# Second RMS norm of a one-core hybrid layer: token sums on partitions, formed by small products behind each output block, in place of a 128-wide sum, root and reciprocal after the last one

## The chip, the cores and the metric

One NeuronCore of one Trainium2 chip runs the whole step as one program. The metric is the device time of that program in microseconds, lower is better; it is the median of several executions. Engines are named as in the profile: PE (TensorE, with PEld its weight loads), DVE (VectorE), ACT (ScalarE), POOL (GpSimd), SP (SyncE, which issues most transfers).

## The reference

The kernel computes one layer on 1024 latent and 128 context tokens of width 1024. The part that matters here is the second norm between the mixer's output projection and the feed-forward:

```python
def rms_norm(x, g):
    xf = x.astype(jnp.float32)
    y = xf * lax.rsqrt(jnp.mean(xf * xf, axis=-1, keepdims=True) + EPS)
    return (y * g.astype(jnp.float32)).astype(x.dtype)
...
    x = x + gt1 * mix                       # mix ends with @ p['w_o']
    xn = rms_norm(x, p['norm2_g']) * (1.0 + sc2) + sh2
    x = x + gt2 * (jnp.square(jax.nn.relu(xn @ p['w_ff1'])) @ p['w_ff2'])
```

Everything is float32.

## The kernel before

Activations lie transposed: channels on the 128 partitions (`KT = 8` blocks of 128 channels), the `T = 1152` tokens along the free dimension, which PE takes in `G = 3` groups of `GN = 384`. `NC = 9` is the number of 128-token chunks. A float32 product is made of three single-pass products on planes of type fp32r: a plane `hi` (the rounded value) and `lo` (the rest), as hi·hi, hi·lo and lo·hi. Weights are split the same way, one 128x1024 block at a time: ACT writes `hi` (L1464, `high`), POOL subtracts to get `lo` (L693, `low`), PE waits for `wl_ok`.

`wave3` (L1149) is one output block: 3 groups of 24 matmuls with 384 columns each, into six PSUM banks used in turn (`WAVE = 6`); banks 6 and 7, which the profile calls `ser`, are free in this stage. The stage concerned has three parts:

1. **Output projection.** Eight output blocks m. After each group DVE adds the gated result to the residual (L1940, writes `x2`). After a block ACT squares it into `sq2[:, m % 2]` (L1490), and DVE adds that to `acc` [128 x 1152] (L1944).
2. **Root.** After the last block PE multiplies `acc` by a matrix of ones, one matmul a group (L1194), which leaves each token's sum on all 128 partitions. ACT takes the root (L1493), DVE the reciprocal of the full 128x1152 tile `rs2` (L1946).
3. **Normalised planes.** For each channel block m: DVE multiplies `x2` by `rs2` (L1953, `xs_ok`), ACT applies scale and shift (L1497, `raw2_ok`) and rounds to `xn2_hi` (L1501, `n2hi_ok`), DVE subtracts to get `xn2_lo` (L1950, `norm_low`, `n2_ok`). `first_hidden` (L1195) on PE takes block k as soon as `n2_ok` reaches k+1: 9 matmuls a block, against the first feed-forward weight block. Then `wave3` goes on with the second weight block, which needs `wl_ok` again.

The order on every engine is the order of the code; there is no scheduler. POOL, in this stage, makes the `lo` plane of one weight block for each output block, then waits for `sum_full`, issues the load of the last norm's weights `gf` (L714) and goes on with `low` for the second feed-forward block.

SBUF tiles that alias are named in the trace by their carrier: `sq2`, `acc`, `rs2`, `gf`, `hsq` appear as `gts`, `xn2_hi`, `xn2_lo`, `xn2_raw` as `xn_hi`, `xn_lo`, `xn_raw`, and the banks as `gbank`, `bank`, `inv`, `ser`, in this order, two of each.

Of the kernel before, what the change touches and what calls it, by code (L numbers as in the profile page):

```python
# [66 lines left out]
N_BRANCH = KT  # L67
# [127 lines left out]
def flow_step(nc, xs, xp, wblocks, pack, packl, vecs, csil_in, consts, gfin, y_out, yp_out, st_out):  # L195
    ctx = ExitStack()
    with ctx:
# [13 lines left out]
        banks = [gbank[:, 0, :], gbank[:, 1, :]]  # L211
# [6 lines left out]
        def sb(st, name, shape, dt=F32):  # L218
            return st.enter_context(nc.sbuf_tensor(name, shape, dt))
# [3 lines left out]
        ident = sb(ctx, "ident", [P, P])  # L223
        bones = sb(ctx, "bones", [P, P])
        ones = sb(ctx, "ones", [P, P])
# [3 lines left out]
        eps_t = sb(ctx, "eps_t", [P, 2])  # L229
# [40 lines left out]
        def sub_tmp(p, d, n, m):  # L270
# [48 lines left out]
        xn2_hi = sb(later, "xn2_hi", [P, KT, T], F32R)  # L319
        x2 = sb(later, "x2", [P, KT, T])  # L320
        xn2_raw = sb(later, "xn2_raw", [P, KT, T])
# [8 lines left out]
        mix_hi = sb(planes, "mix_hi", [P, KT, T], F32R)  # L330
        xa_hi = sb(planes, "xa_hi", [P, KT, T], F32R)
        xn2_lo = sb(planes, "xn2_lo", [P, KT, T], F32R)
        planes.close()
        fin = ExitStack()
# [3 lines left out]
        mix_lo = sb(fin, "mix_lo", [P, KT, T], F32R)  # L338
        gts = sb(fin, "gts", [P, 2, 2, T])
# [4 lines left out]
        sq2 = gts[:, :, 0, :]  # L344
        rs2 = gts[:, 0, 1, :]
        hsq = gts[:, 0, 0, 0:2 * GN].rearrange("p (q t) -> p q t", q=2)
        acc = gts[:, 1, 1, :]
        gf = gts[:, 1, 1, 0:D]
        gate_slots = gts[:, :, :, :].rearrange("p a b t -> p (a b) t")
        yo = xb[:, :, :].rearrange("p k t -> p (k t)")  # L350
        squares = mix_raw[:, :, :].rearrange("p k t -> p (k t)")
        fss = sb(fin, "fss", [P, NC, 2])
        frs = sb(fin, "frs", [P, NC])
        fin.close()
# [6 lines left out]
            tr_full tc_ok p1_full p1_ok dt_full xt_ok tt_ok xtb_ok  # L361
            ur_full ur_ok u_full u_ok s_full y_full s_ok ya_ok yd_ok sf_ok sf_out pl_in0 pl_in1
            mu_full yc_ok ysq_ok var_full std_ok rec_ok spread_full gate_full xa_ok xa_out0 xa_out1 ada_full mrow_ok mt_full ada_ok
            dve_chain pool_chain a_in b_in gt_in0 gt_in1 gt_in2 gt_in3 xh_ok xl_ok xt_in0 xt_in1 wh_ok wl_ok o_full o_free raw_ok hi_ok mix_ok sq_ok acc_ok
            sum_full rs_a2 xs_ok raw2_ok n2hi_ok n2_ok hsq_ok hhi_ok h_ok fin_full fin_sq fin_sum fin_std fin_free fin_out gf_in""".split()
        S = {n: ctx.enter_context(nc.semaphore(n)) for n in names}
        w_full = [ctx.enter_context(nc.semaphore(f"w_full{s}")) for s in range(RING)]
        bon_in = [ctx.enter_context(nc.semaphore(f"bon_in{s}")) for s in range(5)]
# [2 lines left out]
        MIX_FILLS, WO_FILLS, FF_FILLS = 6 * KT, 3 * KT, 3 * (HB + KT)  # L371
# [6 lines left out]
        def cols(cg):  # L378
            return slice(cg * GN, (cg + 1) * GN)
# [234 lines left out]
        def _(pool):  # L614
            ch = Chain(pool, S["pool_chain"])
# [92 lines left out]
            for m in range(KT):  # L708
# [1 line left out]
                    pool.wait_ge(S["o_free"], WAVE + MIX_FILLS + G * m)  # L710
                    pool.dma_start(xts[:, (m + 1) % 2, :], xt_d[m + 1]).then_inc(S[f"xt_in{(m + 1) % 2}"], 16)
                low(2 * N_BRANCH + m + 1)
            pool.wait_ge(S["sum_full"], G)
            pool.dma_start(gf[:], gfin).then_inc(S["gf_in"], 16)  # L714
            with pool.Fori(0, FFE - 1) as i:
                for b in range(2 * HB):
# [11 lines left out]
        def _(pe):  # L728
            def mm(out, lhsT, rhs, start, stop):
                return nc.tensor.matmul(out, lhsT, rhs, start=start, stop=stop)  # L730
# [30 lines left out]
            for c in range(KT):  # L761
                for cg in range(G):
# [3 lines left out]
                    for i in range(G):  # L766
                        ins = nc.tensor.transpose(banks[n % WAVE][:, i * P:(i + 1) * P], x0[:, cg * G + i, c * P:(c + 1) * P], ident[:])
# [5 lines left out]
            for b in range(N_ADA_FIRST):  # L773
                ins = mm(banks[6][:, 2 * b:2 * b + 2], mrow1[:, b // 4, (b % 4) * P:(b % 4 + 1) * P], sel[:], True, True)
# [3 lines left out]
            for c in range(KT):  # L778
                for cg in range(G):
# [4 lines left out]
                    for i in range(G):  # L784
                        ins = nc.tensor.transpose(banks[n % WAVE][:, i * P:(i + 1) * P], xnrm[:, cg * G + i, c * P:(c + 1) * P], ident[:])
# [48 lines left out]
            for k in range(KT):  # L834
                pe.wait_ge(S["xlo_pool" if k % 2 else "xlo_dve"], k // 2 + 1)
                for cg in range(G):
                    ins = product3(banks[FL.bank("l", 0, cg)][:, :GN], *wsp[0], k, cg)
# [7 lines left out]
            for p in range(PAIRS):  # L845
# [7 lines left out]
                for name in AFTER:  # L853
# [10 lines left out]
                    else:  # L864
                        pe.wait_ge(ev["A"], FL.emptied(p, "v")[1])
                        for cg in range(G):
                            o = free_bank(p, name, cg)
                            for i in range(G):
                                t = G * cg + i
                                ins = nc.tensor.transpose(o[:, i * P:(i + 1) * P], vf[:, t * C:(t + 1) * C], ident[:])  # L870
# [278 lines left out]
            def wave3(n0, it, per_it, b, per_b, ks, x, tail=0, ready=None):  # L1149

                if tail == 0:
                    pe.wait_ge(S["wl_ok"], it * per_b + (b + 1))
                hi, lo = wsp[b % 2]
                for cg in range(G):
                    n = n0 + cg
                    pe.wait_ge(S["o_free"], it * per_it + n + 1)
                    if ready:
                        pe.wait_ge(S[ready[0]], it * ready[1] + (ready[2] + cg + 1))
                    for k, kw in enumerate(ks):
                        o = banks[n % WAVE][:, :GN]  # L1160
                        mm(o, hi[:, kw, :], x[0][:, k, cols(cg)], k == 0, False)
                        mm(o, hi[:, kw, :], x[1][:, k, cols(cg)], False, False)
                        ins = mm(o, lo[:, kw, :], x[0][:, k, cols(cg)], False, k == len(ks) - 1)
                    ins.then_inc(S["o_full"], 1)
# [19 lines left out]
                    b = N_BRANCH * x + m  # L1184
                    wave3(G * b, 0, 0, b, 0, range(KT), planes_x)
            pe.wait_ge(S["mix_ok"], G * KT)
            with pe.Fori(0, KT // 4) as i:
                for s in range(4):
                    wave3(MIX_FILLS + 3 * s, i, 12, 2 * N_BRANCH + s, 4, range(KT), (mix_hi, mix_lo))
            n_ff = MIX_FILLS + WO_FILLS  # L1190
            pe.wait_ge(S["o_free"], WAVE + n_ff)
            pe.wait_ge(S["acc_ok"], KT + 1)
            for cg in range(G):
                mm(banks[cg][:, :GN], ones[:], acc[:, cols(cg)], True, True).then_inc(S["sum_full"], 1)  # L1194
            def first_hidden():  # L1195

                pe.wait_ge(S["wl_ok"], 2 * N_BRANCH + KT + 1)
# [24 lines left out]
            for t in range(NC):  # L1222
                if t >= 3:
                    pe.wait_ge(S["fin_free"], 2 * (t - 3) + 2)
                for c in range(KT):
                    ins = nc.tensor.transpose(banks[2 * (t % 3) + c // 4][:, (c % 4) * P:(c % 4 + 1) * P], x2[:, c, t * P:(t + 1) * P], ident[:])
# [5 lines left out]
        def _(act):  # L1232
            A = nc.scalar.activation
# [251 lines left out]
            for m in range(KT):  # L1485
                high(2 * N_BRANCH + m + 1, before=MIX_FILLS + G * m)
                act.wait_ge(S["o_free"], WAVE + MIX_FILLS + G * (m + 1))
                if m >= 2:
                    act.wait_ge(S["acc_ok"], m)
                A(sq2[:, m % 2, :], x2[:, m, :], ACT.Square).then_inc(S["sq_ok"], 1)  # L1490
            for cg in range(G):
                act.wait_ge(S["sum_full"], cg + 1)
                A(rs2[:, cols(cg)], banks[cg][:, :GN], ACT.Sqrt, scale=1.0 / D, bias=eps_t[:, 0:1]).then_inc(S["rs_a2"], 1)  # L1493
            for m in range(KT):
                act.wait_ge(S["xs_ok"], m + 1)
                for a, b, kind in ((0, LAT, 0), (LAT, T, 1)):
                    ins = A(xn2_raw[:, m, a:b], xn2_raw[:, m, a:b], ACT.Identity,  # L1497
                            scale=mul2[:, m, kind:kind + 1], bias=mods[:, 24 + m, kind:kind + 1])
                ins.then_inc(S["raw2_ok"], 1)
                act.wait_ge(S["raw2_ok"], m + 1)  # L1500
                A(xn2_hi[:, m, :], xn2_raw[:, m, :], ACT.Copy).then_inc(S["n2hi_ok"], 1)  # L1501

            n_ff = MIX_FILLS + WO_FILLS

# [27 lines left out]
        def _(dve):  # L1532
            V = nc.vector
            ch = Chain(dve, S["dve_chain"])
# [393 lines left out]
                            if m or cg:  # L1928
                                mix_low(*divmod(G * m + cg - 1, G))
            mix_low(KT - 1, G - 1)  # L1930
            V.memset(acc, 0.0).then_inc(S["acc_ok"], 1)
            with dve.Fori(0, KT // 4) as i:
                for s in range(4):
                    m = 4 * i + s
                    dve.wait_ge(S[f"xt_in{s % 2}"], 32 * i + 16 * (s // 2) + 16)
                    for cg in range(G):
                        n = MIX_FILLS + 3 * s + cg
                        dve.wait_ge(S["o_full"], 12 * i + (n + 1))
                        for a, b, kind in kinds(cg):
                            ins = stt(x2[:, m, a:b], banks[n % WAVE][:, a - cg * GN:b - cg * GN], hgt1[:, m, kind:kind + 1], xts[:, s % 2, a:b], mul, add)  # L1940
                        ins.then_inc(S["o_free"], 1)
                    dve.wait_ge(S["sq_ok"], 4 * i + s + 1)
                    dve.wait_ge(S["acc_ok"], 4 * i + s + 1)
                    V.tensor_tensor(acc, acc, sq2[:, s % 2, :], add).then_inc(S["acc_ok"], 1)  # L1944
            dve.wait_ge(S["rs_a2"], G)
            ch.step(V.reciprocal(rs2, rs2))  # L1946
            ch.settle()
            def norm_low(m):
                dve.wait_ge(S["n2hi_ok"], m + 1)
                V.tensor_tensor(xn2_lo[:, m, :], xn2_raw[:, m, :], xn2_hi[:, m, :].bitcast(F32), sub).then_inc(S["n2_ok"], 1)  # L1950

            for m in range(KT):
                V.tensor_tensor(xn2_raw[:, m, :], x2[:, m, :], rs2, mul).then_inc(S["xs_ok"], 1)  # L1953
                if m >= 2:
                    norm_low(m - 2)
            norm_low(KT - 2)
            norm_low(KT - 1)
            n_ff = MIX_FILLS + WO_FILLS

            def hidden_low(it, n):  # L1960
# [136 lines left out]
```

## Time and profile before

| | us |
|---|---|
| median of 3 runs (lowest to highest) | 2875.52 (2867.75 to 2883.12) |
| the profiled execution, its own time | 2867.05 |
| its span in the trace | 2865.1 |
| PE busy in the span | 2712.8 (95%) |
| DVE, ACT, POOL busy | 1442.3, 823.7, 739.7 |

The span leaves out about 2 us around the first and last instruction. Mean granted TensorE clock is 0.979 of full. The output projection runs from 1904.3 to 2006.4 us of the span, the root and the planes from there to about 2050, the feed-forward from there almost to the end.

### The profile page before, as it was taken

How to read it: one execution, taken by the hardware profiler on the slowest of the kernel's cores; microseconds unless marked ns; L12 is line 12 of the kernel's file. 1: busy time of each engine (PE TensorE's matmuls, PEld its weight loads, DVE VectorE, ACT ScalarE, POOL GpSimd, SP SyncE). 2: the span in 40 equal slices, each digit the busy share in tenths (PEclk: the TensorE clock that was granted, in tenths of full speed). 3: DMA queues.
4: the chain of work that ended last, by engine and by line, in shares of the span. 5: the costliest groups of instructions: out<-in, count | busy, mean ns of one | idle time of the engine just before them, and what ended most of it. 6: DMA issues, size and time to landing. Idle time of an engine off the chain costs nothing.

```text
span 2865.1 us, 65324 instructions
## 1 busy us (share of the span) xinstructions
PE 2712.8 (95%) x27766; PEld 2543.0 (89%) x27766; DVE 1442.3 (50%) x2754; ACT 823.7 (29%) x1542; POOL 739.7 (26%) x883
## 2 busy tenths in 40 slices
PE   3899999999999979999999989999699999999997
PEld 2799999999999967778888879999699999999996
DVE  1355665655845725776666651542633333333334
ACT  3344243343342413333333330211411111111112
POOL 0311111111211215555555532212122212211221
PEclk8899999999999989999999999999899999999999
DMA  7324425425335254444444552212011111111101
GB/s 297 100 69 138 138 72 177 135 68 176 108 103 153 79 169 122 132 122 140 135 136 142 155 209 97 89 50 81 30 45 45 37 44 44 44 37 44 44 29 66
DMA packets 276308, 293.76 MB, mean 103 GB/s; under 512 B 76128, under 2 KB 215776, under 8 KB 275936
## 3 DMA queue, kind: packets, MB, share of 16 engines
q1 hardware_dynamic: 267104, 254.54, 28.9%
q0 software_dynamic: 7200, 28.84, 2.7%
q10 hardware_dynamic: 1760, 6.82, 0.6%
q8 instruction: 191, 3.13, 0.4%
q14 instruction: 53, 0.43, 0.0%
HBM read 198.76 MB, written 91.36 MB: 101 GB/s over the span
## 4 chain that ended last, share of the span: by engine, by line
PE 92%; issue 3%; DVE 3%; DMA 2%; ACT 1%; SPq 1%; POOL 0%; DVEq 0%; POOLq 0%; ACTq 0%
PE gbank L730 26%; PE inv L730 23%; PE bank L730 23%; PE ser L730 17%; PE inv L916 1%; DMA ring<-in_wblocks 1%; PE bank L903 1%; DVE gmat L1756 1%; DMA xt_d<-xt_s 0%; DVE xr L1588 0%; DVE xb L1993 0%; POOL wsp L693 0%; SPq L543 0%; SPq L544 0%; DVE yf L1816 0%
## 5 line engine op out<-in xcount | busy, mean ns | idle before, releaser
L693 POOL TENSOR_TENSOR wsp<-ring,wsp 128x1024 fp32r<-128x1024 f32 x88 | 215.8, 2453 | 842.2 <-ACT wsp L1464 819.1
L624 POOL TENSOR_TENSOR wsp<-ring,wsp 128x1024 fp32r<-128x1024 f32 x67 | 174.8, 2609 | 746.7 <-ACT wsp L1260 746.7
L730 PE MATMUL gbank<-xn_hi,wsp 128*128 128x384 f32 x1312 | 348.3, 339 | 18.9 <-DVE xn_lo L1950 18.2
L730 PE MATMUL bank<-xn_hi,wsp 128*128 128x384 f32 x1312 | 345.3, 337 | 0.4 <-POOL wsp L693 0.4
L730 PE MATMUL inv<-xn_hi,wsp 128*128 128x384 f32 x1312 | 343.5, 337 | 0.0
L730 PEld LDWEIGHTS gbank<-xn_hi,wsp 128*128 128x128 f32 x1312 | 239.5, 189 | 23.7 <-issue 15.7
L730 PEld LDWEIGHTS bank<-xn_hi,wsp 128*128 128x128 f32 x1312 | 238.3, 188 | 2.5 <-POOL wsp L693 0.7
L730 PEld LDWEIGHTS inv<-xn_hi,wsp 128*128 128x128 f32 x1312 | 237.9, 188 | 1.8 <-POOL wsp L624 1.1
L1464 ACT ACTIVATE wsp<-ring 128x1024 fp32r<-128x1024 f32 x88 | 92.6, 1052 | 465.0 <-PE inv L730 385.5
L730 PE MATMUL ser<-xn_hi,wsp 128*128 128x384 f32 x816 | 218.8, 342 | 5.4 <-DVE xr L1588 5.4
L730 PE MATMUL bank<-xn_lo,wsp 128*128 128x384 f32 x656 | 220.5, 336 | 1.4 <-issue 1.4
L730 PE MATMUL gbank<-xn_lo,wsp 128*128 128x384 f32 x656 | 221.1, 337 | 0.0
L730 PE MATMUL inv<-xn_lo,wsp 128*128 128x384 f32 x656 | 220.3, 336 | 0.0
L730 PE MATMUL gbank<-ub 64*64 64x128 f32 (+1 forms) x3456 | 183.1, 316 | 21.4 <-DVE gmat L1756 12.4
L1756 DVE TENSOR_TENSOR gmat<-gbank,gmask 128x1024 f32<-128x1024 f32 x144 | 175.4, 1218 | 44.8 <-PE gbank L730 44.8
L730 PE MATMUL gbank<-mix_lo,wsp 128*128 128x384 f32 x832 | 159.9, 335 | 0.0
L730 PE MATMUL inv<-mix_lo,wsp 128*128 128x384 f32 x832 | 159.9, 335 | 0.0
L730 PE MATMUL bank<-mix_lo,wsp 128*128 128x384 f32 x832 | 159.9, 335 | 0.0
L730 PEld LDWEIGHTS ser<-xn_hi,wsp 128*128 128x128 f32 x816 | 150.5, 190 | 7.4 <-DVE xr L1588 5.6
L730 PEld LDWEIGHTS bank<-mix_lo,wsp 128*128 128x128 f32 x832 | 145.6, 188 | 0.0
L730 PEld LDWEIGHTS inv<-mix_lo,wsp 128*128 128x128 f32 x832 | 145.6, 188 | 0.0
L730 PEld LDWEIGHTS gbank<-mix_lo,wsp 128*128 128x128 f32 x832 | 145.6, 188 | 0.0
(380 smaller groups left out, 5295.0 us busy)
## 6 DMA issues: line engine op xcount, KB each, us to landing
ring<-in_wblocks SPq DMA_DIRECT2D x195, 512.0 KB, 3.6
ub<-op_d SPq DMA_DIRECT2D x144, 256.0 KB, 2.8
op_d<-ar SPq DMA_DIRECT2D x32, 576.0 KB, 5.4
op_d<-bk SPq DMA_DIRECT2D x32, 576.0 KB, 6.2
vb<-v_d SPq DMA_DIRECT2D x144, 64.0 KB, 3.0
xt_d<-xt_s POOLq DMA_DIRECT2D x8, 576.0 KB, 3.2
x_d<-zero SPq DMA_DIRECT2D x8, 576.0 KB, 6.8
v_d<-vn SPq DMA_DIRECT2D x8, 576.0 KB, 6.8
```

Source lines behind the costliest of these rows:

```text
L624: GT(wsp[s % 2][1][:], ring[(N_ADA_RING + s) % RING][:], wsp[s % 2][0][:].bitcast(F32), ALU.subtract).then_inc(S["wsplit_lo"], 1)
L693: nc.gpsimd.tensor_tensor(wsp[b % 2][1][:], ring[(N_MIX0 + b) % RING][:], wsp[b % 2][0][:].bitcast(F32), ALU.subtract).then_inc(S["wl_ok"], 1)
L730: return nc.tensor.matmul(out, lhsT, rhs, start=start, stop=stop)
L903: ins = nc.tensor.transpose(banks[3][:, y * P:(y + 1) * P], ub[v % LOADS][:, y // 2, 2 + y % 2, :], ident[:])
L916: ins = nc.tensor.transpose(inv[:, 0, x * P:(x + 1) * P], xt[:, place_of(v), :, :].rearrange("p h t -> p (h t)"), ident[:])
L1464: A(wsp[b % 2][0][:], ring[slot][:], ACT.Copy).then_inc(S["wh_ok"], 1)
L1756: V.tensor_tensor(gmat[v % SETS][:, d, :, :, :].rearrange("p h x t -> p h (x t)"), gbank[:, :, :], gmask[:, d:d + 1, :].to_broadcast([P, 2 ...
```

## The change

- The squares of block m are no longer added up by DVE. PE multiplies each 128-token chunk of `sq2` (as the stationary operand) by two columns of ones: nine matmuls a block, accumulated over the eight blocks in bank 6, which leave the sum of token p of chunk t on partition p in column 2t (`token_sums`). They stand one block behind: the sums of block m-1 come after the matmuls of block m. PE's loop of two turns is written out.
- ACT takes the root of those nine columns (128x9) and DVE the reciprocal of 128x9 (`rtok`).
- PE spreads `rtok` back over partitions: nine matmuls with a column of `rtok` repeated 128 times as stationary operand and the identity as moving one, into banks 3 to 5; ACT copies these to `rs2`.
- The rounding to `xn2_hi` is done by ACT for even m and by DVE (`norm_high`) for odd m; the subtraction to `xn2_lo` is done by POOL for all m. The load of `gf` on POOL stands behind these eight subtractions.

```diff
-        acc = gts[:, 1, 1, :]
+        rtok = sb(fin, "rtok", [P, NC])
...
-            pool.wait_ge(S["sum_full"], G)
+            for m in range(KT):
+                pool.wait_ge(S["n2hd_ok" if m % 2 else "n2hi_ok"], m // 2 + 1)
+                nc.gpsimd.tensor_tensor(xn2_lo[:, m, :], xn2_raw[:, m, :], xn2_hi[:, m, :].bitcast(F32), ALU.subtract).then_inc(S["n2_ok"], 1)
             pool.dma_start(gf[:], gfin).then_inc(S["gf_in"], 16)
...
-            with pe.Fori(0, KT // 4) as i:
-                for s in range(4):
-                    wave3(MIX_FILLS + 3 * s, i, 12, 2 * N_BRANCH + s, 4, range(KT), (mix_hi, mix_lo))
+            def token_sums(m):
+
+                pe.wait_ge(S["sq_ok"], m + 1)
+                for t in range(NC):
+                    ins = mm(banks[6][:, 2 * t:2 * t + 2], sq2[:, m % 2, t * P:(t + 1) * P], ones[:, 0:2], m == 0 and t == 0, m == KT - 1 and t == NC - 1)
+                ins.then_inc(S["ss_full"], 1)
+
+            for m in range(KT):
+                wave3(MIX_FILLS + 3 * m, 0, 0, 2 * N_BRANCH + m, 0, range(KT), (mix_hi, mix_lo))
+                if m:
+                    token_sums(m - 1)
+            token_sums(KT - 1)
             n_ff = MIX_FILLS + WO_FILLS
             pe.wait_ge(S["o_free"], WAVE + n_ff)
-            pe.wait_ge(S["acc_ok"], KT + 1)
+            pe.wait_ge(S["rtok_ok"], 1)
             for cg in range(G):
-                mm(banks[cg][:, :GN], ones[:], acc[:, cols(cg)], True, True).then_inc(S["sum_full"], 1)
+                for i in range(G):
+                    t = G * cg + i
+                    ins = mm(banks[3 + cg][:, i * P:(i + 1) * P], rtok[:, t:t + 1].to_broadcast([P, P]), ident[:], True, True)
+                ins.then_inc(S["sum_full"], 1)
...
                 if m >= 2:
-                    act.wait_ge(S["acc_ok"], m)
+                    act.wait_ge(S["ss_full"], m - 1)
                 A(sq2[:, m % 2, :], x2[:, m, :], ACT.Square).then_inc(S["sq_ok"], 1)
+            act.wait_ge(S["ss_full"], KT)
+            A(rtok[:], banks[6][:, 0:2 * NC:2], ACT.Sqrt, scale=1.0 / D, bias=eps_t[:, 0:1]).then_inc(S["rs_a2"], 1)
             for cg in range(G):
                 act.wait_ge(S["sum_full"], cg + 1)
-                A(rs2[:, cols(cg)], banks[cg][:, :GN], ACT.Sqrt, scale=1.0 / D, bias=eps_t[:, 0:1]).then_inc(S["rs_a2"], 1)
+                A(rs2[:, cols(cg)], banks[3 + cg][:, :GN], ACT.Copy).then_inc(S["rs_ok"], 1)
...
-                act.wait_ge(S["raw2_ok"], m + 1)
-                A(xn2_hi[:, m, :], xn2_raw[:, m, :], ACT.Copy).then_inc(S["n2hi_ok"], 1)
+                if m % 2 == 0:
+                    act.wait_ge(S["raw2_ok"], m + 1)
+                    A(xn2_hi[:, m, :], xn2_raw[:, m, :], ACT.Copy).then_inc(S["n2hi_ok"], 1)
...
-                    V.tensor_tensor(acc, acc, sq2[:, s % 2, :], add).then_inc(S["acc_ok"], 1)
-            dve.wait_ge(S["rs_a2"], G)
-            ch.step(V.reciprocal(rs2, rs2))
-            ch.settle()
-            def norm_low(m):
-                dve.wait_ge(S["n2hi_ok"], m + 1)
-                V.tensor_tensor(xn2_lo[:, m, :], xn2_raw[:, m, :], xn2_hi[:, m, :].bitcast(F32), sub).then_inc(S["n2_ok"], 1)
-
+            dve.wait_ge(S["rs_a2"], 1)
+            V.reciprocal(rtok[:], rtok[:]).then_inc(S["rtok_ok"], 1)
+            def norm_high(m):
+                dve.wait_ge(S["raw2_ok"], m + 1)
+                V.tensor_copy(xn2_hi[:, m, :], xn2_raw[:, m, :]).then_inc(S["n2hd_ok"], 1)
+
+            dve.wait_ge(S["rs_ok"], G)
             for m in range(KT):
                 V.tensor_tensor(xn2_raw[:, m, :], x2[:, m, :], rs2, mul).then_inc(S["xs_ok"], 1)
-                if m >= 2:
-                    norm_low(m - 2)
-            norm_low(KT - 2)
-            norm_low(KT - 1)
+                if m >= 3 and m % 2:
+                    norm_high(m - 2)
+            norm_high(KT - 1)
```

How this moves instructions is seen best on three engines. On PE, where one output block ends and the next begins, the changed program has (the first row is the last product of a block, `ones,gts` are the token sums):

```order
L732 MATMUL inv<-mix_lo,wsp 128x384
L732 MATMUL inv<-mix_hi,wsp 128x384
L732 MATMUL ser<-ones,gts 128x2 x9
L732 MATMUL gbank<-mix_hi,wsp 128x384
L732 MATMUL gbank<-mix_lo,wsp 128x384
```

Before, the row of nine is not there and the next block follows at once. Such a row of nine stands between two blocks six times (the sums of blocks 0 to 5, each behind the block after it). The sums of blocks 6 and 7 stand together behind the last block:

```order
L732 MATMUL inv<-mix_hi,wsp 128x384
L732 MATMUL ser<-ones,gts 128x2 x18
L732 MATMUL bank<-ident,rtok 128x128 x3
L732 MATMUL inv<-ident,rtok 128x128 x6
L732 MATMUL gbank<-xn_hi,wsp 128x384
```

where before there stand the three matmuls of the ones matrix:

```order
L730 MATMUL gbank<-gts,ones 128x384 x2
L730 MATMUL bank<-gts,ones 128x384
L730 MATMUL gbank<-xn_hi,wsp 128x384
```

On DVE after the last residual add, first before and then changed (`xn_raw<-x,gts` are the multiplications by the root's reciprocal, `CAST` is `norm_high`):

```order
L1946 RECIPROCAL gts<-gts 128x1152
L1953 TENSOR_TENSOR xn_raw<-x,gts 128x1152 x3
L1950 TENSOR_TENSOR xn_lo<-xn_raw,xn_hi 128x1152
L1953 TENSOR_TENSOR xn_raw<-x,gts 128x1152
```

```order
L1960 RECIPROCAL rtok<-rtok 128x9
L1967 TENSOR_TENSOR xn_raw<-x,gts 128x1152 x4
L1963 CAST xn_hi<-xn_raw 128x1152
L1967 TENSOR_TENSOR xn_raw<-x,gts 128x1152 x2
L1963 CAST xn_hi<-xn_raw 128x1152
L1967 TENSOR_TENSOR xn_raw<-x,gts 128x1152 x2
L1963 CAST xn_hi<-xn_raw 128x1152 x2
```

The subtractions have left DVE and four casts stand there. On POOL, ahead of the second feed-forward weight block, the changed program has:

```order
L715 TENSOR_TENSOR xn_lo<-xn_raw,xn_hi 128x1152 x8
L716 DMA gts<-in_gfin 128x1024
L717 UNCONDITIONAL_BRANCH
L717 ISA
L693 TENSOR_TENSOR wsp<-ring,wsp 128x1024
```

Before, the DMA and the L693 row stand there without the eight subtractions.

## Rows read from the trace of the kernel before

**Rows 1.** The page: the span.
```profile
span 2865.1 us, 65324 instructions
```
**Rows 2.** Stretches: us; busy PE, PEld, DVE, ACT, POOL (instructions); clock, DMA share, GB/s.
```profile
1904.30:2006.40 102.10, 102.02 (x576) 101.70 (x576) 25.53 (x38) 14.89 (x15) 24.13 (x14) 1.00 0.23 76
...
2008.00:2050.00 42.00, 21.37 (x83) 16.93 (x84) 32.01 (x21) 25.21 (x30) 3.16 (x2) 0.72 0.04 13
```
**Rows 3.** Timeline of PE, 2006 to 2050: start, length, instruction, idle before.
```profile
2006.05 0.34 PE L730 MATMUL inv<-mix_hi,wsp 128*128 128x384 f32 x1
...
2010.02 2.90 PE L730 MATMUL gbank<-gts,ones 128*128 128x384 f32 x4 [3.63 <-DVE gts L1944]
2012.72 1.49 PE L730 MATMUL bank<-gts,ones 128*128 128x384 f32 x2
...
2049.14 0.44 PE L730 MATMUL bank<-xn_hi,wsp 128*128 128x384 f32 x1 [0.40 <-POOL wsp L693]
```
**Rows 4.** Timelines of ACT and DVE, 2006 to 2050.
```profile
2007.32 1.16 ACT L1490 ACTIVATE gts<-x 128x1152 f32<-128x1152 f32 x1 [10.61 <-DVE x L1940]
2011.68 0.58 ACT L1493 ACTIVATE gts<-gbank,eps_t 128x384 f32<-128x384 f32 x1 [3.20 <-PE gbank L730]
...
2026.36 1.61 ACT L1497 ACTIVATE xn_raw<-xn_raw,mods,mul 128x1024 f32<-128x1024 f32 x2
2028.00 1.17 ACT L1501 ACTIVATE xn_hi<-xn_raw 128x1152 fp32r<-128x1152 f32 x1
...
2014.86 7.35 DVE L1946 RECIPROCAL gts<-gts 128x1152 f32<-128x1152 f32 x1 [4.98 <-ACT gts L1493]
2022.24 3.89 DVE L1953 TENSOR_TENSOR xn_raw<-x,gts 128x1152 f32<-128x1152 f32 x3
...
2045.49 1.36 DVE L1950 TENSOR_TENSOR xn_lo<-xn_raw,xn_hi 128x1152 fp32r<-128x1152 f32 x1 [1.36 <-ACT xn_hi L1501]
```
**Rows 5.** Timeline of POOL, 2006 to 2075.
```profile
2014.50 0.57 POOL L714 DMA_DIRECT2D gts<-in_gfin  x1 [15.08 <-PE bank L730]
...
2053.87 2.40 POOL L693 TENSOR_TENSOR wsp<-ring,wsp 128x1024 fp32r<-128x1024 f32 x1 [4.78 <-ACT wsp L1464]
```
**Rows 6.** Float32 matmuls of two columns: eight weight loads; PE and clock in the prologue's.
```profile
1190.85 0.97 PEld L730 LDWEIGHTS bank<-sel,mrow 128*128 128x128 f32 x8 [0.17 <-issue]
...
70.00:73.00 3.00, 3.00 (x28) 1.00 0.19 75
73.00:73.50 0.50, 0.50 (x6) 0.71 0.00 0
...
76.50:77.00 0.50, 0.50 (x6) 0.88 0.00 0
```
**Rows 7.** Small operations like the added ones: ACT and DVE on 128x9.
```profile
L1303 ACT ACTIVATE emid<-mid 128x9 f32<-128x9 f32 x16 | 3.1, 193 | 0.0
...
L1558 DVE RECIPROCAL rs<-rs x1: 205/205/205, 43.5 to 43.5; 128x9 f32<-128x9 f32 x1
```
**Rows 8.** PE's clock after its last output matmul (windows of 0.5 us).
```profile
2008.50:2009.00 0.50, 0.00 (x0) 0.57 0.00 0
```
**Rows 9.** Timelines of POOL, then of DVE, in the prologue.
```profile
81.35 2.63 POOL L629 TENSOR_TENSOR xn_lo<-xr,xn_hi 128x1152 fp32r<-128x1152 f32 x1 [12.78 <-DVE xr L1588]
83.94 3.47 POOL L624 TENSOR_TENSOR wsp<-ring,wsp 128x1024 fp32r<-128x1024 f32 x1
...
83.17 2.02 DVE L1579 TENSOR_TENSOR xn_lo<-xr,xn_hi 128x1152 fp32r<-128x1152 f32 x1
```
**Rows 10.** A DVE cast, and a DVE op with one SBUF input (min/median/max ns).
```profile
L1566 DVE CAST gmask<-cst x1: 686/686/686, 50.1 to 50.1; 128x1024 bf16<-128x1024 f32 x1
...
L1701 DVE TENSOR_SCALAR kk<-kk x8: 760/761/762, 186.4 to 976.2; 128x1152 f32<-128x1152 f32 x8
```
**Rows 11.** DVE's timeline where POOL's split of 803.03 to 805.42 runs.
```profile
803.03 2.39 POOL L624 TENSOR_TENSOR wsp<-ring,wsp 128x1024 fp32r<-128x1024 f32 x1 [13.95 <-ACT wsp L1260]
...
803.92 1.52 DVE L1612 TENSOR_SCALAR half<-pk 128x4 f32<-128x4 f32 x1
```

More of the change, by code:

```diff
@@ L363, in flow_step @@
             mu_full yc_ok ysq_ok var_full std_ok rec_ok spread_full gate_full xa_ok xa_out0 xa_out1 ada_full mrow_ok mt_full ada_ok
-            dve_chain pool_chain a_in b_in gt_in0 gt_in1 gt_in2 gt_in3 xh_ok xl_ok xt_in0 xt_in1 wh_ok wl_ok o_full o_free raw_ok hi_ok mix_ok sq_ok acc_ok
-            sum_full rs_a2 xs_ok raw2_ok n2hi_ok n2_ok hsq_ok hhi_ok h_ok fin_full fin_sq fin_sum fin_std fin_free fin_out gf_in""".split()
+            dve_chain pool_chain a_in b_in gt_in0 gt_in1 gt_in2 gt_in3 xh_ok xl_ok xt_in0 xt_in1 wh_ok wl_ok o_full o_free raw_ok hi_ok mix_ok sq_ok ss_full
+            sum_full rs_a2 rtok_ok rs_ok xs_ok raw2_ok n2hi_ok n2hd_ok n2_ok hsq_ok hhi_ok h_ok fin_full fin_sq fin_sum fin_std fin_free fin_out gf_in""".split()
         S = {n: ctx.enter_context(nc.semaphore(n)) for n in names}
@@ L1930, in _ @@
             mix_low(KT - 1, G - 1)
-            V.memset(acc, 0.0).then_inc(S["acc_ok"], 1)
             with dve.Fori(0, KT // 4) as i:
@@ L1941, in _ @@
                         ins.then_inc(S["o_free"], 1)
-                    dve.wait_ge(S["sq_ok"], 4 * i + s + 1)
-                    dve.wait_ge(S["acc_ok"], 4 * i + s + 1)
-                    V.tensor_tensor(acc, acc, sq2[:, s % 2, :], add).then_inc(S["acc_ok"], 1)
-            dve.wait_ge(S["rs_a2"], G)
-            ch.step(V.reciprocal(rs2, rs2))
-            ch.settle()
-            def norm_low(m):
-                dve.wait_ge(S["n2hi_ok"], m + 1)
-                V.tensor_tensor(xn2_lo[:, m, :], xn2_raw[:, m, :], xn2_hi[:, m, :].bitcast(F32), sub).then_inc(S["n2_ok"], 1)
+            dve.wait_ge(S["rs_a2"], 1)
[4 more added lines that the diff above has]
+            dve.wait_ge(S["rs_ok"], G)
             for m in range(KT):
                 V.tensor_tensor(xn2_raw[:, m, :], x2[:, m, :], rs2, mul).then_inc(S["xs_ok"], 1)
-                if m >= 2:
-                    norm_low(m - 2)
-            norm_low(KT - 2)
-            norm_low(KT - 1)
+                if m >= 3 and m % 2:
+                    norm_high(m - 2)
+            norm_high(KT - 1)
             n_ff = MIX_FILLS + WO_FILLS
```

## The prediction

> **What bounds the kernel now.** I read the table of stretches first. Over the eight output blocks PE is busy 102.02 of 102.10 us, at full clock, and its weight loads 101.70; DVE, ACT and POOL are under a quarter [rows 2]. So in this stretch each microsecond of PE work lengthens the kernel by one, and work taken from DVE is worth nothing. In the next one PE is busy for half of the time and its clock is at 0.72: here a chain through the other engines sets the end. I then read that chain in the timelines, with t = 0 at the end of PE's last output matmul, 2006.05 + 0.34 = 2006.39 [rows 3]:
> - The last block is squared by 2008.48, t = 2.1 [rows 4]; DVE adds it, PE starts on the ones matrix at 2010.02 [rows 3].
> - ACT takes three roots, and DVE the reciprocal from 2014.86, 7.35 us [rows 4].
> - The first multiplication by it starts at 2022.24, t = 15.85. Then each channel block passes ACT in 1.61 + 1.17 us, more than DVE's multiplication and subtraction need; the last subtraction ends at 2045.49 + 1.36 = 2046.85, t = 40.5 [rows 4].
> - PE starts its first full feed-forward block at 2049.14, t = 42.75; the row names POOL's weight split as what released it [rows 3].
>
> Whatever moves this last point moves the end, since PE is the bound from there on.
>
> **The change, part by part.**
> *Token sums between blocks.* The nearest row is the float32 matmul of 128x128 weights with two columns. Each is executed as two passes, each with its own weight load. Eight loads take 0.97 us [rows 6], the last 0.19 of it its own length: (0.97 - 0.19)/7 = 0.11 us apart. In the prologue 28 passes fill 3.0 us, 0.107 each [rows 6]. Nine matmuls are 18 passes: 18 x 0.107 = 1.9 us. Two columns instead of 384 save nothing here, because the loads set the pace. Six such groups stand between blocks: 6 x 1.92 = **+11.5 us**, all on the bound. At 0.97/8 a pass it would be 13.1. Their wait costs nothing: the squares of block m-1 are ready about 2 us into block m. DVE's eight additions to `acc` and its memset, which go, were hidden behind PE; only the last one was on the chain.
>
> *From the last block to the first multiplication.* The sums of block 6 (1.9 us) run while the last block is gated and squared (2.1), so they are free. Sums of block 7: 2.2 to 4.1. On to ACT 0.3 (as from 2010.02 + 1.35 to 2011.68 [rows 3, 4]), root of 128x9 0.19, reciprocal of 128x9 0.205 [rows 7], with hand-overs t = 4.95. Then nine matmuls of 128 columns. At half clock two of 384 columns took 2012.72 - 2010.02 = 2.7 us [rows 3], so 1.35/3 = 0.45 each, 4.05 in all; at full clock 2.0. I take half clock: the clock fell about 2.2 us after the last output matmul [rows 8], and in the prologue it fell while two-column matmuls were running, after 3.2 us of them [rows 6]. Here 4 us of them and a pause stand ahead. So 9.0, then 0.3 and a copy of at most 0.58 [rows 4]: multiplications start at t = 9.95 against 15.85, **-5.9 us**. It is what is left of the 7.35 of the reciprocal, the addition and the ones matrix.
>
> *Planes.* Here the work moves to POOL, where a 128x1152 subtraction takes 2.63 us [rows 9] against DVE's 1.36, and that isn't all. Where POOL and DVE both have an operation with two SBUF inputs, one waits for the other's end: DVE's subtraction at 83.17 took 2.02 us, until POOL's had ended at 83.98 and its own time had passed; POOL's next, started at 83.94, took 3.47 instead of 2.40, for it waited for DVE's [rows 5, 9]. DVE's `TENSOR_SCALAR` on four columns, begun 0.9 us into a POOL split, ended with it, after 1.52 us [rows 11]; that form has one SBUF input and runs 1152 columns in 0.76 [rows 10], and the added cast is like it: 0.686 for 1024 columns, so 0.77. So three kinds of work exclude each other: 8 multiplications at (3.89 - 1.35)/2 = 1.27 [rows 4], 8 subtractions at 2.63, 4 casts at 0.77: 10.2 + 21.0 + 3.1 = 34.3 us, and one of them is nearly always ready (ACT needs 8 x 1.61 + 4 x 1.17 = 17.6). The last plane is ready at t = 44.25, against 40.5: the stage gets slower by more than the root won. If the cast ran at one column a cycle and excluded nothing, the sum is 31.2.
>
> The Trainium skill, "SBUF — State Buffer", section "Who interferes with whom", states that copies and casts in a two-port mode, and DVE operations with two SBUF inputs, contend with GpSimd for a port pair held for a whole instruction. By that rule the 34.3 stands and the 31.2 falls; the trace agrees for the two-input form and for `TENSOR_SCALAR`, and no row here shows a float32 to fp32r cast.
>
> *Behind it on POOL.* The load of `gf` (0.57) and the split of the second feed-forward block (2.40) [rows 5] used to run before and beside the last subtraction on DVE; now both are queued behind POOL's own eighth. PE's next block waits for it: 44.25 + 0.57 + 2.40 + hand-overs = 47.35 against 42.75, **+4.6 us** for the whole chain (the -5.9 is within it). PE itself needs 9 x 102.02/576 = 1.6 us for its nine matmuls on the last plane [rows 2] and isn't late.
>
> **Sum:** 11.5 + 4.6 = +16.1 us. On the profiled execution, 2867.05 (span 2865.1 [rows 1]), that is 2883.2; it is the lowest of the runs, so I add it to the median instead: 2875.52 + 16.1 = 2891.6, 0.56% more.
>
> **The rivals.**
> 1. *POOL and DVE run side by side* (not slower by what can be told). Then POOL starts at 9.95 + 1.27 + 1.61 + 1.17 = 14.1 with hand-overs and ends 21.0 later, at 35.1; with `gf` and the split 38.2, -4.5 against now, and the total is 11.5 - 4.5 = +7.0, 2882.5. Rows 9 speak against it; for it only that other pairs of tiles are concerned. It decides from 1.8 us less exclusion than I count on, since 14.4 us is 0.5%. Chance 0.14. With only the cast free: +13.0, 2888.5; chance 0.1.
> 2. *The clock falls between the output blocks.* Two-column matmuls didn't hold it in the prologue [rows 6]; it was low from about 73.2 to 76.6, 3.4 us, and work at half clock loses half of that, 1.7. Once in each gap: 6 x 1.7 = +10.2, total 26.3, 2901.8. Against it: 1.9 us stand between two blocks of 12.7 us of dense work. Chance 0.15, for some of it.
> 3. *The clock holds up to the spread:* -2.0, total 14.1, 2889.6. Chance 0.1.
> 4. *The sums are hidden.* Then only +4.6 stays, 2880.1. Against it: the weight loads of the blocks fill 101.70 of 102.10 us, so there is no room to load ahead. Chance 0.04.
>
> The Trainium skill, "TensorE: Matmul & The Clock Gate", section "Step-by-step: what each phase is for", has the queue pull weight loads ahead of running matmuls, which is the rule that rival 4 would live by; rows 2 and 6 show no gain from it for back-to-back loads.
>
> **How the numbers follow.** My forecast with all its steps has 0.44, and it is the likeliest: 2892 us. About 0.5% is what a measurement of this kernel can tell from no change, 14.4 us here, and the three runs before lie 15 us apart, so a true +16 can be measured on either side of it. The forecast gives 0.32 to slower, rival 2 all, the cast and rival 3 a half, rival 1 and 4 next to nothing: slower 0.57, same 0.4. Faster by 14 us would need hidden sums and no exclusion, and 10 us more: 0.03. The range reaches from rival 1 with some scatter, 2879, to rival 2, 2903.
>
> **What would show each step.** PE rows of nine two-column matmuls of about 1.9 us between blocks, and an output stretch of about 113.6 us instead of 102.1; the clock there at 1.00 (0.9 or less: rival 2). The first multiplication at t = 10. Multiplications and casts on DVE, while POOL subtracts, of 2 to 4 us instead of 1.35 and 0.77, and POOL's subtractions with idle time between them. The last of these at t = 44, and PE released by the POOL split at t = 47. The prediction is wrong if the 18 passes take under 1 us, if POOL's eight follow each other at 2.6 us from t = 14, or if the feed-forward stretch changes its length.

## The result and the profile after

The changed kernel takes 2890.05 us in the median of 14 runs (2884.79 to 2904.41) against 2876.11 us of the kernel before (14 runs, 2867.75 to 2885.87). The ratio of the record is 1.0051, 95% interval 1.0036 to 1.0066: half a percent slower, 13.9 us by the medians. The forecast was 2892 us, +16.1.

The profiled execution took 2885.17 us. The page's span and busy times answer to [rows 1]:

```profile
span 2883.3 us, 65589 instructions
PE 2736.2 (95%) x27922; PEld 2567.6 (89%) x27922; DVE 1426.2 (49%) x2741; ACT 819.7 (28%) x1539; POOL 763.4 (26%) x891
```

PE has 156 more rows of matmul passes (27922 against 27766): (72 + 9) x 2 = 162 of the new forms, less the six of the ones matrix. The timeline of PE: the first and last output matmul, the first row of a gap, the last sums, the spread, the last plane and the next full block (it answers to [rows 3]):

```profile
1901.04 0.44 PE L732 MATMUL gbank<-mix_hi,wsp 128*128 128x384 f32 x1 [2.39 <-DVE mix_lo L1924]
...
1927.81 1.93 PE L732 MATMUL ser<-ones,gts 128*128 128x2 f32 x16
1929.60 0.42 PE L732 MATMUL gbank<-mix_hi,wsp 128*128 128x384 f32 x1
...
2014.42 0.34 PE L732 MATMUL inv<-mix_hi,wsp 128*128 128x384 f32 x1
...
2016.90 3.12 PE L732 MATMUL ser<-ones,gts 128*128 128x2 f32 x18 [0.24 <-ACT gts L1505]
2020.72 1.62 PE L732 MATMUL bank<-ident,rtok 128*128 128x128 f32 x6 [0.70 <-DVE rtok L1960]
...
2058.30 0.44 PE L732 MATMUL gbank<-xn_hi,wsp 128*128 128x384 f32 x1 [0.79 <-POOL xn_lo L715]
...
2061.23 0.45 PE L732 MATMUL bank<-xn_hi,wsp 128*128 128x384 f32 x1 [1.09 <-POOL wsp L693]
```

t = 0 is 2014.42 + 0.34 = 2014.76. The output stretch is 113.72 us long (102.02 before), the next full block starts at t = 46.47 (42.75). DVE and POOL in the planes, which answer to [rows 4, 5]:

```profile
2020.36 0.21 DVE L1960 RECIPROCAL rtok<-rtok 128x9 f32<-128x9 f32 x1 [4.71 <-ACT rtok L1507]
2025.44 5.16 DVE L1967 TENSOR_TENSOR xn_raw<-x,gts 128x1152 f32<-128x1152 f32 x4 [4.87 <-ACT gts L1510]
2031.20 2.50 DVE L1963 CAST xn_hi<-xn_raw 128x1152 fp32r<-128x1152 f32 x1 [0.60 <-ACT xn_raw L1514]
2033.62 5.07 DVE L1967 TENSOR_TENSOR xn_raw<-x,gts 128x1152 f32<-128x1152 f32 x2
2038.61 3.20 DVE L1963 CAST xn_hi<-xn_raw 128x1152 fp32r<-128x1152 f32 x1
```

```profile
2029.73 3.35 POOL L715 TENSOR_TENSOR xn_lo<-xn_raw,xn_hi 128x1152 fp32r<-128x1152 f32 x1 [23.93 <-ACT xn_hi L1519]
2033.78 7.41 POOL L715 TENSOR_TENSOR xn_lo<-xn_raw,xn_hi 128x1152 fp32r<-128x1152 f32 x2 [0.70 <-DVE xn_hi L1963]
...
2049.96 8.28 POOL L715 TENSOR_TENSOR xn_lo<-xn_raw,xn_hi 128x1152 fp32r<-128x1152 f32 x3 [0.70 <-DVE xn_hi L1963]
2058.20 0.57 POOL L716 DMA_DIRECT2D gts<-in_gfin  x1
2058.79 2.38 POOL L693 TENSOR_TENSOR wsp<-ring,wsp 128x1024 fp32r<-128x1024 f32 x1
```

Read the second and fourth DVE rows together: the first four multiplications, which POOL doesn't hold up, take 5.16 us; the next two, with POOL at work, take 5.07. Whichever engine starts first goes on at its own pace and the other waits: the eight multiplications took 1.34 us at least, 1.35 in the median and 3.80 at most. The first cast takes 2.50 us, from 2031.20 to 2033.70, while the four casts' shortest is 0.746. POOL's pair takes 7.41 us instead of 2 x 2.63; only the last three, with little left for DVE to do, come near it (8.28).

### The profile page after: what moved, and what is told of

It reads as the page before. It is cut to its first block, busy times and chain, and to the rows that moved or that the text cites. A ratio compares the mean times of both kernels' runs of the same rounds, so it can differ in the third digit from the quotient of the medians.

```text
span 2883.3 us, 65589 instructions
## 1 busy us (share of the span) xinstructions
PE 2736.2 (95%) x27922; PEld 2567.6 (89%) x27922; DVE 1426.2 (49%) x2741; ACT 819.7 (28%) x1539; POOL 763.4 (26%) x891
## 4 chain that ended last, share of the span: by engine, by line
PE 92%; DVE 3%; DMA 2%; issue 1%; ACT 1%; SPq 1%; POOL 0%; DVEq 0%; POOLq 0%; ACTq 0%
PE gbank L732 25%; PE inv L732 23%; PE bank L732 23%; PE ser L732 18%; PE inv L918 1%; DMA ring<-in_wblocks 1%; PE bank L905 1%; DVE gmat L1774 1%; DVE xr L1606 0%; DVE xb L2006 0%; DMA xt_d<-xt_s 0%; DVE xn_raw L1967 0%; DVE xn_hi L1963 0%; POOL xn_lo L715 0%; DVE yf L1834 0%
## 5 line engine op out<-in xcount | busy, mean ns | idle before, releaser
L693 POOL TENSOR_TENSOR wsp<-ring,wsp 128x1024 fp32r<-128x1024 f32 x88 | 213.4, 2425 | 816.8 <-ACT wsp L1479 793.1
```

What stands on the lines that cost most here:

```text
L693: nc.gpsimd.tensor_tensor(wsp[b % 2][1][:], ring[(N_MIX0 + b) % RING][:], wsp[b % 2][0][:].bitcast(F32), ALU.subtract).then_inc(S["wl_ok"], 1)
```

## The experiments

The clearest measure is taken from the traces, since the times of one kernel's runs lie up to 20 us and more apart (what is known of that is in the last section). For each kernel: the output stretch, t of the first multiplication, of the end of the last plane and of the next full feed-forward block, and as "both" the time from the first output matmul to that block. What the change does to the time lies in "both". The profiled execution is one for each kernel, and the output stretch alone is uncertain by some 2.6 us: where nothing stands between the blocks it is 100.9 to 103.5 us long. Two things differ between executions there: the spacing of the dense matmuls (0.1746 us in most of them, 0.1766 in before and sums_tail), and whether 3.4 us near its beginning passed at half clock (changed, sums_tail, sums_twice, psum_mult, tail_back, tail_back_psum_early), which costs 1.7 us. The three times counted from the end of that stretch are free of this. The last column is the record's ratio of the runs, which is not the quotient of the two medians (for planes_only that would be 1.0036).

| kernel | output stretch | first mult. | last plane | full block | both | median (runs) | ratio to before, 95% |
|---|---|---|---|---|---|---|---|
| before | 102.0 | 15.9 | 40.5 | 42.75 | 144.8 | 2876.11 (14) | |
| changed | 113.7 | 10.7 | 43.5 | 46.5 | 160.2 | 2890.05 (14) | 1.0051 [1.0036, 1.0066] |
| planes_back | 112.3 | 11.5 | 36.1 | 38.4 | 150.7 | 2881.72 (12) | 1.0015 [0.9994, 1.0036] |
| planes_only | 100.9 | 15.5 | 48.3 | 51.6 | 152.5 | 2885.98 (12) | 1.0019 [0.9998, 1.0041] |
| sums_tail | 103.5 | 10.6 | 43.4 | 46.4 | 149.9 | 2879.42 (12) | 0.9994 [0.9971, 1.0016] |
| sums_twice | 140.6 | 10.3 | 43.1 | 46.1 | 186.7 | 2925.96 (1) | |
| psum_mult | 114.3 | 8.0 | 36.9 | 39.9 | 154.2 | 2881.87 (12) | 1.0010 [0.9992, 1.0028] |
| tail_back | 102.4 | 9.2 | 33.8 | 36.1 | 138.5 | 2862.79 (11) | 0.9969 [0.9953, 0.9985] |
| tail_back_psum | 100.9 | 7.4 | 33.7 | 36.0 | 136.9 | 2861.86 (12) | 0.9960 [0.9945, 0.9976] |
| tail_back_psum_early | 102.4 | 6.6 | 32.6 | 34.3 | 136.7 | 2864.36 (12) | 0.9980 [0.9961, 0.9999] |

The kernel before ran again beside each group: 2875.49 us (35 runs) beside planes_back, planes_only, sums_tail and psum_mult, 2871.78 (29 runs) beside sums_twice and the last three.

**planes_back: the work on the planes where it was.** On the changed kernel:

```diff
-                if m % 2 == 0:
-                    act.wait_ge(S["raw2_ok"], m + 1)
-                    A(xn2_hi[:, m, :], xn2_raw[:, m, :], ACT.Copy).then_inc(S["n2hi_ok"], 1)
+                act.wait_ge(S["raw2_ok"], m + 1)
+                A(xn2_hi[:, m, :], xn2_raw[:, m, :], ACT.Copy).then_inc(S["n2hi_ok"], 1)
...
-            for m in range(KT):
-                pool.wait_ge(S["n2hd_ok" if m % 2 else "n2hi_ok"], m // 2 + 1)
-                nc.gpsimd.tensor_tensor(xn2_lo[:, m, :], xn2_raw[:, m, :], xn2_hi[:, m, :].bitcast(F32), ALU.subtract).then_inc(S["n2_ok"], 1)
+            pool.wait_ge(S["sum_full"], G)
...
-                if m >= 3 and m % 2:
-                    norm_high(m - 2)
-            norm_high(KT - 1)
+                if m >= 2:
+                    norm_low(m - 2)
+            norm_low(KT - 2)
+            norm_low(KT - 1)
```

`norm_low` is DVE's subtraction `xn2_lo = xn2_raw - xn2_hi` for one plane; the wait on `sum_full` keeps POOL's transfer of `gf` behind the last read of the squares.

Expected:

> The changed kernel with the planes as before: ACT rounds all eight blocks, DVE subtracts, POOL only waits for the spread; token sums, root and spread as changed. Counted from the end of the last output matmul (t = 0), the multiplications start at 10.7 in the changed kernel. Theory (work moved to POOL excludes DVE's): last plane at 10.7 + 24.65 = 35.3, next full feed-forward block at 37.6 instead of 46.5 (changed) and 42.75 (before); output stretch still 11.5 us longer than before; total about 6 us above before. Rival (the planes are slow in the changed kernel for another reason, such as the later start of the split or the clock): the block stays at 43 or later, total 11 us or more above before.

Measured: from the first multiplication to the last plane 24.6 us, as before, against 32.8 in the changed kernel; the full block at 38.4. PE's row, with the last plane released by DVE 2.2 us ahead of it:

```profile
2051.15 0.45 PE L730 MATMUL gbank<-xn_hi,wsp 128*128 128x384 f32 x1 [0.89 <-DVE xn_lo L1960]
...
2053.39 0.44 PE L730 MATMUL bank<-xn_hi,wsp 128*128 128x384 f32 x1 [0.40 <-POOL wsp L693]
```

The rival falls: with the sums and the root left as changed, moving the work back alone gives 8.1 us in the tail. The block comes 0.8 us later than expected, as the multiplications do: here the clock fell at 2017.2 us, at the beginning of block 7's sums, whose 18 passes took 3.91 us.

**planes_only: the same move alone, on the kernel before.** The diff is that of the change for ACT's copies, POOL's subtractions and DVE's casts, and nothing else.

> The kernel before with only the planes moved (ACT and DVE round in turn, POOL subtracts, gf behind it); sum, root and reciprocal on 128x1152 as before. Theory: multiplications start at t = 15.85 as before, last plane 32.8 later at 48.7 (before 40.5), next full block at 51.6 (before 42.75): 9 us above before, output stretch unchanged. Rival (the move is neutral by itself): block at 43 to 45, total within 2 us of before.

Measured: last plane 32.8 us after the first multiplication, the full block at 51.6, +8.8 us in the tail. At the end it is PE that holds the block: its clock was low again (0.50 from 2051.7 to 2058.5), the nine matmuls on the last plane ended only then, 0.3 us after POOL's split. So the move costs the same on either kernel, 8 to 9 us. The medians show +10.5 us, the ratio is 1.0019, and its interval just reaches no change.

**sums_tail: no token sums between the blocks.**

```diff
             for m in range(KT):
                 wave3(MIX_FILLS + 3 * m, 0, 0, 2 * N_BRANCH + m, 0, range(KT), (mix_hi, mix_lo))
-                if m:
-                    token_sums(m - 1)
-            token_sums(KT - 1)
+            pe.wait_ge(S["acc_ok"], KT)
+            token_sums(acc, True, False)
+            pe.wait_ge(S["sq_ok"], KT)
+            token_sums(sq2[:, (KT - 1) % 2, :], False, True).then_inc(S["ss_full"], 1)
```

(and DVE adds `sq2` to `acc` for blocks 0 to 6, as the kernel before does for all eight).

> The changed kernel, but no token sums between the output blocks: DVE adds the squares of blocks 0 to 6 to one tile as before, and PE forms the token sums of that tile and of block 7's squares behind the last block (18 matmuls, as the changed kernel has there). Theory: the output stretch is back at 102 us, the rest as in the changed kernel (block at 46.5), total about 4 us above before, 11.5 below the changed kernel. Rival (the sums were partly hidden, the stretch is longer for another reason): less than 6 us below the changed kernel.

Measured: the stretch is 103.5 us, 10.2 shorter than the changed kernel's, and the tail is the changed one's to 0.1 us. Both had 3.4 us at half clock near their beginning, but the dense matmuls were 0.1766 us apart here and 0.1745 there in most blocks, which over 576 is about 1.3 us: with like spacing the six groups are worth 11.5. The 18 matmuls behind the last block are free in their first half: they run while the last block is gated and squared, and the multiplications start at 10.6 all the same.

**psum_mult: DVE multiplies from PSUM.**

```diff
-            for cg in range(G):
-                act.wait_ge(S["sum_full"], cg + 1)
-                A(rs2[:, cols(cg)], banks[3 + cg][:, :GN], ACT.Copy).then_inc(S["rs_ok"], 1)
...
-                V.tensor_tensor(xn2_raw[:, m, :], x2[:, m, :], rs2, mul).then_inc(S["xs_ok"], 1)
+                for cg in range(G):
+                    if m == 0:
+                        dve.wait_ge(S["sum_full"], cg + 1)
+                    ins = V.tensor_tensor(xn2_raw[:, m, cols(cg)], x2[:, m, cols(cg)], banks[3 + cg][:, :GN], mul)
+                ins.then_inc(S["xs_ok"], 1)
```

> The changed kernel, but DVE multiplies by the reciprocal roots straight from the three PSUM banks (three operations of 384 columns a block, one SBUF input each), and ACT's three copies go. POOL's subtractions and the casts stay. Theory (two SBUF inputs on DVE exclude POOL): the first block's product is ready at 10.8 instead of 12.1, POOL's subtractions are held up by the four casts alone: last plane at 35 to 38, block at 38 to 41, 6 to 8 us below the changed kernel. Rival (the exclusion is not by SBUF inputs, any DVE operation holds POOL up, or nothing does): only the earlier start is won, block at 45, 1 to 2 us below.

Measured: last plane at 36.9, block at 39.9, 6.6 us earlier than in the changed kernel. Of these, 1.3 are the earlier start (the first block's product is complete at 10.7 instead of 12.0), 5.3 the planes. The timeline of POOL:

```profile
2031.28 2.63 POOL L715 TENSOR_TENSOR xn_lo<-xn_raw,xn_hi 128x1152 fp32r<-128x1152 f32 x1 [22.61 <-ACT xn_hi L1516]
2034.60 19.97 POOL L715 TENSOR_TENSOR xn_lo<-xn_raw,xn_hi 128x1152 fp32r<-128x1152 f32 x7 [0.70 <-DVE xn_hi L1960]
```

And four rows of DVE that ran at the same time:

```profile
2032.75 1.77 DVE L1960 CAST xn_hi<-xn_raw 128x1152 fp32r<-128x1152 f32 x1 [0.23 <-ACT xn_raw L1511]
...
2036.30 1.00 DVE L1966 TENSOR_TENSOR xn_raw<-x,inv 128x384 f32<-128x384 f32 x2
2037.23 0.74 DVE L1960 CAST xn_hi<-xn_raw 128x1152 fp32r<-128x1152 f32 x1
...
2041.21 2.52 DVE L1960 CAST xn_hi<-xn_raw 128x1152 fp32r<-128x1152 f32 x1 [0.45 <-ACT xn_raw L1511]
```

A multiplication with one input in PSUM goes on at full speed beside POOL's subtraction (1.00 us for two of 384 columns; all 24 took 0.54 to 0.55 each), and POOL's go on too (seven in 19.97 us; the median of the eight is 2.67 us). The casts still exclude POOL: the first ends at 2034.52, 0.6 us after POOL's first subtraction (2033.91); the one at 2037.23 comes first and takes its own 0.74 us, and the subtraction beside it takes 3.27, the longest of the eight. So the exclusion is between POOL's subtraction and DVE operations with two SBUF inputs, or the SBUF-to-SBUF cast, as the Trainium skill has it ("SBUF — State Buffer", "Who interferes with whom"). The rival falls. This run made the operations shorter as well, 384 columns instead of 1152, and none was made with short ones from SBUF. But a row of the kernel before, in the feed-forward, shows that shortness is not the reason. There the square of a 128x384 tile in SBUF, a product with two SBUF inputs and 0.56 us in the median of its 96, ran beside POOL's split of 2053.87 to 2056.27 [rows 5] and took 2.49:

```profile
2054.19 2.49 DVE L1974 TENSOR_TENSOR gts<-gts 128x384 f32<-128x384 f32 x1
```

**sums_twice: each of the six groups between blocks issued twice**, the extra one into a bank that nothing reads.

> The changed kernel with the nine two-column matmuls of each of the six gaps between output blocks issued twice (the extra set writes to a bank that nothing reads). Theory (18 passes cost 1.9 us on the bound, the clock holds): output stretch 113.7 + 11.5 = 125 us, clock in it 0.98 or more, the tail as in the changed kernel. Rival (the clock falls when two-column matmuls take a larger part): the stretch is longer than 127 us and the clock below 0.95 in it.

Here the rival holds. The timeline of PE has the 36 passes between two blocks as one row:

```profile
1933.37 4.08 PE L732 MATMUL ser<-ones,gts 128*128 128x2 f32 x36
```

They end at 1937.45 and still ran at full clock (1.00 from 1933 to 1938); from 1938 to 1944 the granted clock was 0.72. Two gaps later, in the row that began at 1969.81, it fell before the row's end: 5.27 us for the same 36 passes. Four stretches of 4 us there, with PE's time in the stretch, its busy time with the number of matmuls, the clock, the DMA share and GB/s:

```profile
1968.00:1972.00 4.00, 4.00 (x33) 1.00 0.00 0
1972.00:1976.00 4.00, 4.00 (x20) 0.56 0.45 147
1976.00:1980.00 4.00, 4.00 (x16) 0.59 0.42 131
1980.00:1984.00 4.00, 4.00 (x25) 1.00 0.00 0
```

The mean clock over the whole stretch is 0.88. The output stretch is 140.6 us, 15.4 above the 125.2 (113.7 + 11.5) that passes alone would give. About 3.4 us at half clock at its beginning are not the sums' doing, as the changed kernel had them too. With 18 passes in a gap, 1.93 us, the clock was 1.00 in the changed kernel from 1905.5 to 2014.7. So rival 2 of the prediction is a real mechanism, one group of nine matmuls a gap away; this rests on one execution, in which the clock fell in or just behind each of the six gaps. The tail is the changed kernel's (block at 46.1).

**tail_back, tail_back_psum, tail_back_psum_early: what can be kept.** tail_back is sums_tail with the planes of planes_back; tail_back_psum adds the multiplication from PSUM; the last one adds an early split of the first feed-forward weights (ACT ahead of its root, POOL ahead of `gf`):

```diff
+            high(2 * N_BRANCH + KT + 1, before=MIX_FILLS + WO_FILLS)
             act.wait_ge(S["ss_full"], 1)
...
+            low(2 * N_BRANCH + KT + 1)
             pool.wait_ge(S["sum_full"], G)
```

with the first turn of the feed-forward loop on ACT and POOL written out without that block.

> Token sums only behind the last block (DVE adds up blocks 0 to 6) and the planes as before: what is left of the change is the 18 two-column matmuls behind the last block, the root and reciprocal of 128x9 and the spread. Theory (the two terms add): output stretch 102 us, next full feed-forward block at t = 38.4 against 42.75, 4 us below before in the changed stretches, 0.15% of the time, which the medians can hardly tell. Rival (DVE's adding for block 6 delays the token sums, or the earlier end is given back): block at 41 or later.

> As tail_back, and DVE multiplies straight from PSUM without ACT's three copies. Theory: multiplications start at t = 8, the first block's product is ready 2 us earlier than in tail_back, ACT's pace of 2.72 us a block sets the rest: last plane at 34, full block at 36.3, 6 us below before in the changed stretches. Rival (DVE's three operations and the subtraction, 2.75 us a block, become the bound): last plane at 35 or later.

> As tail_back_psum, and ACT rounds and POOL splits the second feed-forward weight block while PE forms the last token sums, ahead of the planes. Theory: the next full block no longer waits for POOL but starts when PE has done the last plane's nine matmuls, 1.6 us after it: t = 35.9 at most, 0.5 us below tail_back_psum, 7 us below before, 0.24%. Rival (the rounding delays ACT's root, since ACT has only 3.6 us free there): the multiplications start 0.5 us or more later and nothing is won.

Measured: tail_back's block stands at 36.1 instead of the 38.4 expected. The token sums behind the last block, in tail_back and then in tail_back_psum:

```profile
2007.51 4.36 PE L731 MATMUL ser<-ones,gts 128*128 128x2 f32 x36
```

```profile
2002.83 5.17 PE L731 MATMUL ser<-ones,gts 128*128 128x2 f32 x36
```

In tail_back there is no pause between the sums of `acc` and those of block 7, and the clock fell only behind them (at 2012.3), so they end at 4.2 instead of 6.1 in planes_back; part of the spread ran at full clock, too: multiplications at 9.2 instead of 11.5. The tail is 6.6 us shorter than before's, against the 4.4 that planes_back had let me expect, and those 2.3 us come mostly from when the clock fell. "Both" is 6.2 us below before, and the ratio 0.9969 [0.9953, 0.9985]. tail_back_psum starts to multiply 1.8 us earlier, but ACT starts at 10.5 against 10.6 and the block stands at 36.0: in that execution the clock fell inside the sums (the 36 passes took 5.17 us), the whole spread ran at half clock, and the first block needs all three banks. The two can't be told apart. The early split does what it should in the trace: PE goes from the last plane into the next block without a row of waiting, at 34.3; from the last plane to the block it takes 1.7 us instead of 2.3, and the rest is an earlier end of the sums. Its median is the highest of the three all the same, inside the scatter. The lowest ratio is tail_back_psum's, 0.9960 of before, 95% 0.9945 to 0.9976; its interval and tail_back's overlap for the most part.

## Why the prediction was right, step by step

- **Token sums between blocks, +11.5: right.** A group takes 1927.81 - 0.16 to 1929.60, 1.9 us; exactly, the matmuls on its two sides start 2.10 us apart in all six gaps, where dense ones are 0.17 apart, so 1.93 are added each time. The stretch grew by 11.7, but that it comes so close is luck, for two accidents cancel: the changed kernel's execution began it at half clock (0.50 from 1902 to 1904, and on to about 1905.3, some 1.7 us), and its dense matmuls were spaced closer than before's. sums_tail confirms the term by removing it (10.2 us, 11.5 with like spacing).
- **First multiplication at t = 9.95: 10.7.** Three errors. I had the clock fall only for the spread; it fell inside the sums of block 7 (1.00 to 2017.9, 0.50 after it), whose 18 passes took 3.12 us instead of 1.9. Two hand-overs to ACT that I had put at 0.3 us are 0.04 by the trace (the root starts at 2020.06, the sums end at 2020.02; the last copy at 2024.92, behind the spread's end at 2024.88). And the copy on ACT took 0.49, not 0.58. Term mis-sized by 0.7 us: -5.2 instead of -5.9.
- **Planes, 34.3 us from first multiplication to last plane: 32.8.** Exclusion as described; over by 1.5 us, because an operation that has waited for the other engine finishes in less than its own time after it (a cast begun at 2031.20 ended 0.6 us after POOL's end at 2033.08) and the casts take 0.746. The rows of the prologue had shown as much: DVE's subtraction there ended at 85.19, 1.21 us after POOL's end at 83.98, and not after its whole 1.36. psum_mult shows which operations exclude each other, planes_back and planes_only the price: 8 us.
- **`gf` and the split behind it, 3.1: 3.0**, from 43.5 to 46.5. For the tail: +3.7 instead of +4.6.
- **Sum: +16.1; in the two stretches 160.2 - 144.8 = +15.4**, in the medians +13.9 (10 to 19 by the ratio's interval). In the tail two errors partly cancel, too: the multiplications start 0.7 us later than forecast, and the planes take 1.5 less.
- **Rival 1 (no exclusion):** fell. **Rival 2 (clock):** not in this kernel, but one step away. **Rival 3 (clock holds up to the spread):** fell. **Rival 4 (sums hidden):** fell.
- **"The prediction is wrong if the feed-forward stretch changes its length"** was a bad test. In the profiled executions it did, by 6.1 us (from the full block to the end of the span, 822.1 against 816.0), most likely not through the change: see the last section.

## What to carry to other kernels

On the engine that is the bound, count weight loads as well as columns: nine float32 matmuls of two columns cost 1.9 us, as their 18 weight loads come 0.107 us apart whatever the two columns need, and six groups of them ate twice what the short reciprocal won. A sum that another engine has been making for nothing should stay there, and only its last step, 128x9 instead of 128x1152, be reformed: that half of the change made the tail 4 to 7 us shorter, depending on when the clock fell. Before work is shared with POOL, ask which of DVE's operations have two SBUF inputs or are SBUF-to-SBUF casts; where they must stay, POOL's share isn't in parallel, and PSUM inputs on DVE are a way out.

## What the runs showed of the hardware that I had not expected

**The dense matmuls have three spacings, at the same granted clock of 1.00.** The chain's rows, 48 matmuls each, in the feed-forward of three kernels (before, changed, planes_back):

```profile
2577.72 8.32 PE inv L730 x48
```

```profile
2593.88 8.38 PE inv L732 x48
```

```profile
2592.13 8.48 PE inv L730 x48
```

That is 0.1733, 0.1747 or 0.1767 us a matmul. A spacing held through the whole feed-forward of an execution, and was another in other stages of the same one (before: 8.32 on the feed-forward, 8.48 on the output blocks); within the output blocks it also changed from one block to the next. The feed-forward has 4608 such matmuls. From the full block to the end of the span it took 816.0 to 816.3 us in the executions with the first spacing, 822.1 with the second and 830.3 to 831.1 with the third: 6 us between the first two and some 15 between the first and the third. This is the size of the scatter of the runs (sums_tail: four runs at 2866 to 2869, five at 2877 to 2882, three at 2887 to 2889). Of the ten profiled executions three had 8.32 there (before, tail_back, tail_back_psum), one 8.38 (the changed kernel) and six 8.48. tail_back_psum_early, with the same matmul loop as tail_back_psum, is among the six, and the runs of one kernel scatter by as much: its profiled execution took 2871.16 us and its fastest run 2858.19, while all that stands ahead of the output blocks varied by under 6 us among the ten. So I take the spacing as a property of an execution and not of a kernel, which is argued and not shown. What sets it wasn't found out. It is why a change of 5 us is judged here by a stretch of the trace, and by the median of a dozen runs only in sign.

**Twice the two-column matmuls cost more than twice.** Over the kernel before, six groups of 18 passes lengthened the output stretch by 11.7 us (113.7 - 102.0), six of 36 by 38.6 us (140.6 - 102.0); the granted clock was 1.00 between the blocks of the one and 0.88 on average over the stretch of the other (one execution).
